# The even layer's norm as a factor of its products, with raw x turned between the first of them, and the output projection's parts two places sooner

## Chip, cores and metric

One core of one Trainium2 chip runs the whole program. The metric is the time of one execution on the device in microseconds (us). TensorE is the matrix engine, ScalarE, VectorE and GpSimd (POOL) work elementwise, and SyncE (SP) issues nearly all DMAs. All data is fp32.

## What is computed

The program runs two blocks on x of 256 tokens by 1024 features. The first block is a gated delta rule mixer (8 query/key heads, 16 value heads of 128, chunks of 64, in both directions) with an output projection of 2048 to 1024, then a mixture of 32 experts, then a gated embedding. The second block is an even layer and an odd layer. What the change touches:

```python
# end of the first block: gated embedding
x = x + sigmoid(layernorm(x) @ pe_w_gate) * (p @ pe_w_proj)
# even layer
xn = rmsnorm(x, g_norm)              # x * rsqrt(mean(x*x) + 1e-6) * g_norm
p = xn @ w_in
q, k, v, o, z_a, gates, u, z_b = _split(p, EVEN_SPLITS)
qk = silu(causal_conv(concat([q, k]), conv_w))       # 4 taps per channel
gates = gates + b_if
# delta rule's mixer ends with
return o.reshape(bsz, seq, GDN_VAL_WIDTH) @ w_out
```

The norm of the even layer is one number for each token, r = rsqrt(mean(x*x) + 1e-6), and one factor for each feature, g_norm. Since r is the same for all features of a token, (r x g) W = r ((x g) W).

## The kernel before

Each engine has its own instruction stream, written out by hand in order; semaphores (`Signal`) tie them together. A "unit" is a weight tile of 1024 by 256, 1 MB, that SP fills into one of 20 slots; `fill` waits until the products of the slot's last unit are done, and `multiplied[s]` and `arrived[s]` count products and fills of slot s. The sixteen slots beyond the first few lie in the arena, in `yt` and in `xt`. One unit's product with all tokens is 16 matmuls of 128x128 by 256 columns; in fp32 each shows as two instructions, so a unit is 32 instructions in the trace, and a 128x128 transpose is two.

**Delta rule** (`gdn_tensor`). The loop over h runs 9 times (h = 0 to 8). In round h TensorE does the levels of head h's triangular inverse and its projections (`project_half`) and, woven in, the four state steps of head h-1: `solve`, `attend`, `add_state`, `read_state`. Each step waits for a copy by ScalarE or VectorE, and the work written between the steps fills those waits. The last round, h = 8, has no projections left; in their place stand the 16 parts of the first half of the output projection: `out_part(cg, part)` takes 4 matmuls (8 instructions) of column group cg; parts 0 and 1 belong to the first token tile, 2 and 3 to the second. Eleven places have 1, 1, 1, 1, 2, 1, 1, 2, 1, 1 and 4 parts, the 4 behind the last `attend`. After the loop comes `out_rest` with the second half of the input rows, with `turn_out(7)` between.

At the end of round 7 the order is solve(6, 3), attend(6, 3), `turn_v(7)` (v of head 7 turned, for the first solve of round 8), with no projection between them, since heads 8 and 9 do not exist. `out_part` waits for the slot's fill, and for the bank's last reader (`out_free`): for the first parts ScalarE's copy of z.

**Experts** (`moe`). 96 units of weights stream through the slots; the rest of the slots' fills follows the products. Then `embed`: gate products in four column groups over two token tiles (banks 4 to 7), p's projection in banks 0 to 3; ScalarE takes the sigmoid of each group, VectorE multiplies and adds to x, group by group (`embedded(1)` to `embedded(4)`).

**Even layer** (`even`). In order: ScalarE waits for `embedded(4)`, squares x with a sum (two instructions), takes Ln and Exp; VectorE makes xn = x r; TensorE turns xn with 16 transposes through two banks (`turn_tensor`), ScalarE copies them out to `xt` with the feature factor g_norm (`turn_scalar`); TensorE makes the gates' products (16 matmuls with 8 columns each) in bank 4, and then 8 units of q and k, one bank each (banks 0 to 3, twice). ScalarE copies each bank to `raw`, VectorE runs the 4 taps of the convolution over it (8 instructions a unit), ScalarE takes silu. VectorE's and ScalarE's steps for the forget gates run beside the units. Then 4 units of v (`project`), the a rows, the scores, and 16 units for z_a, o, z_b and u (`project_on`), each copied by ScalarE with one instruction of 128x512 (Silu for z, Copy for the rest). Everything afterwards stays as it is.

## Time and profile before

| | us |
|---|---|
| three runs | 1200.20, 1204.52, 1205.24 |
| median | 1204.52 |
| the profiled execution's own time | 1200.51 |
| its span | 1199.2 |
| mean granted TensorE clock | 0.95 |

The profiled execution's times below are counted from the start of its span; 1.3 us lie around it. TensorE's rows are split into matmuls (PE) and the weight loads that overlap them (PEld). A row's duration of a matmul contains the time through the pipeline, so a series is read by the step from one start to the next. "idle before <-releaser" is what the engine waited for.

### The profile page before, as it was taken

Reading aid. Unit: us, or ns where it says so; the run is one execution under the profiler, and the core shown is the slowest. Engines: PE = TensorE matmul, PEld = TensorE weight load, DVE = VectorE, ACT = ScalarE, POOL = GpSimd, SP = SyncE. Lnnn points to the kernel's source line nnn. Section 1 sums busy time; section 2 is a strip of 40 time slices with the busy share of each in tenths; the row PEclk is TensorE's granted clock in tenths of the full one; section 3 lists DMA queues with packets and bytes.
Section 4 is the critical chain, followed back from the end, with each engine's and each line's share of the span. In section 5 each row is a group of like instructions: output and inputs, shape, how many; then the busy total and the mean of one; then the engine's idle time right before and its main releaser. Section 6 shows DMA issues by size and latency. Waiting matters only on the chain.

```text
span 1199.2 us, 24296 instructions
## 1 busy us (share of the span) xinstructions
PE 1085.5 (91%) x10653; PEld 831.2 (69%) x10653; DVE 387.6 (32%) x927; ACT 354.8 (30%) x965; POOL 44.3 (4%) x47
## 2 busy tenths in 40 slices
PE   7999999999899989877677979999999798999989
PEld 6776777767667885333233868888888587777877
DVE  2555555555542242110001424411001100074760
ACT  2654655545553221100001131111002500133440
POOL 0110000000000000000000000000000000023000
PEclk9999999999899999898888969999999899799989
DMA  6233233223226568999999413334443234432211
GB/s 257 78 128 116 72 117 118 86 101 122 93 72 267 190 225 346 419 421 422 421 421 419 182 56 140 141 140 140 142 164 115 71 140 177 107 140 71 90 51 36
DMA packets 39887, 210.41 MB, mean 175 GB/s; under 512 B 5200, under 2 KB 14288, under 8 KB 15840
## 3 DMA queue, kind: packets, MB, share of 16 engines
q1 hardware_dynamic: 39776, 208.79, 46.0%
q8 instruction: 87, 1.43, 0.5%
q14 instruction: 24, 0.20, 0.1%
HBM read 207.66 MB, written 1.11 MB: 174 GB/s over the span
## 4 chain that ended last, share of the span: by engine, by line
PE 76%; SPq 10%; DVE 5%; DMA 4%; ACT 4%; issue 2%; DVEq 0%; ACTq 0%
PE ps L448 9%; SPq L235 9%; PE ps L2230 9%; PE ps L250 7%; PE ps L2148 5%; PE ps L451 4%; PE ps L764 3%; DMA arena<-in_wu 2%; PE ps L2611 2%; PE ps L2519 2%; PE ps L2026 2%; PE ps L775 2%; PE ps L2550 2%; PE ps L504 2%; PE ps L470 2%
## 5 line engine op out<-in xcount | busy, mean ns | idle before, releaser
L448 PE MATMUL ps<-xt,slots 128*128 128x256 f32 x512 | 128.0, 397 | 0.0
L2230 PE MATMUL ps<-slots,xt 128*128 128x256 f32 x512 | 110.7, 379 | 0.0
L448 PEld LDWEIGHTS ps<-xt,slots 128*128 128x128 f32 x512 | 95.1, 195 | 19.8 <-issue 7.5
L2230 PEld LDWEIGHTS ps<-slots,xt 128*128 128x128 f32 x512 | 97.2, 190 | 13.2
L1533 PE MATMUL ps<-arena 128*32 128x512 f32 x280 | 54.1, 666 | 22.8 <-DMA arena<-in_wu 9.1
L451 PE MATMUL ps<-slots,xt 128*128 128x256 f32 x256 | 65.1, 398 | 0.0
L250 PE MATMUL ps<-slots,yt 128*128 128x256 f32 x256 | 57.3, 388 | 0.9 <-ACT yt L280 0.9
L2148 PE MATMUL ps<-xt,slots 128*128 128x256 f32 x256 | 57.1, 387 | 0.0
L1087 DVE SCALAR_TENSOR_TENSOR arena<-arena 128x256 f32<-128x256 f32 x128 | 56.3, 486 | 0.3
L250 PEld LDWEIGHTS ps<-slots,yt 128*128 128x128 f32 x256 | 49.8, 195 | 8.4 <-ACT yt L280 1.3
L2148 PEld LDWEIGHTS ps<-xt,slots 128*128 128x128 f32 x256 | 49.7, 195 | 7.0
L451 PEld LDWEIGHTS ps<-slots,xt 128*128 128x128 f32 x256 | 46.9, 193 | 10.8 <-issue 4.3
L1533 PE MATMUL ps<-slots,arena 128*32 128x512 f32 x160 | 44.4, 708 | 6.0 <-DMA xt<-in_wu 6.0
L1533 PEld LDWEIGHTS ps<-arena 128*32 128x32 f32 x280 | 14.8, 120 | 50.4 <-issue 50.4
L2916 POOL TENSOR_TENSOR arena<-arena 128x512 f32<-128x512 f32 (+1 forms) x8 | 17.8, 2259 | 732.1 <-DVE arena L2811 732.1
L2375 DVE SCALAR_TENSOR_TENSOR arena<-ps,arena 128x256 f32<-128x256 f32 x8 | 3.2, 478 | 108.3 <-ACT arena L2285 108.3
L2278 ACT ACTIVATE arena<-ps 128x512 f32<-128x512 f32 x16 | 9.6, 597 | 93.8 <-PE ps L2230 93.8
L1633 ACT ACTIVATE arena<-ps 128x256 f32<-128x256 f32 x8 | 3.1, 385 | 115.1 <-PE ps L1533 115.1
L1309 POOL TENSOR_TENSOR arena<-arena 128x256 f32<-128x256 f32 x32 | 24.8, 776 | 312.1 <-ACT arena L830 194.0
L266 PE MATMUL ps<-cst,arena 128*128 128x128 f32 x84 | 17.5, 370 | 20.5 <-DVE arena L2316 7.7
L1854 DVE TENSOR_TENSOR arena<-arena,ps 128x256 f32<-128x256 f32 x8 | 3.4, 422 | 92.8 <-ACT arena L1633 92.8
L2550 PE MATMUL ps<-slots,xt 128*128 128x256 f32 x128 | 31.8, 393 | 1.2 <-ACT arena L2718 1.2
(386 smaller groups left out, 1853.9 us busy)
## 6 DMA issues: line engine op xcount, KB each, us to landing
slots<-in_wu SPq DMA_DIRECT2D x114, 1024.0 KB, 4.8
arena<-in_wu SPq DMA_DIRECT2D x58, 1024.0 KB, 26.1
yt<-in_wu SPq DMA_DIRECT2D x10, 1024.0 KB, 26.1
xt<-in_wu SPq DMA_DIRECT2D x4, 1024.0 KB, 27.7
arena<-bias_rows SPq DMA_DIRECT2D x1, 2048.0 KB, 14.7
arena<-delta_rows SPq DMA_DIRECT2D x14, 128.0 KB, 7.6
xt<-in_xt SPq DMA_DIRECT2D x2, 512.0 KB, 5.3
x<-in_x SPq DMA_DIRECT2D x1, 1024.0 KB, 8.2
```

The lines of the kernel that those rows point to most:

```text
L235: SP.dma_start(self.slot(slot), self.ins["wu"][unit]).then_inc(*self.arrived[slot].up())
L250: q = M.matmul(self.bank(base + cg, UC, t * UC), lhs[:, h * KT + k, t * P:(t + 1) * P], self.slot(s)[:, k, :], start=(t == 0 and k == 0 an ...
L448: q = M.matmul(bank(n, T), self.slots[:, s, k, n * P:(n + 1) * P], self.xt[:, k, :], start=(k == 0), stop=(k == KT - 1))
L451: q = M.matmul(bank(n, UC), folded(k, n), self.slots[:, s, k, :], start=(k == 0), stop=(k == KT - 1))
L470: q = M.matmul(ps[p, 3, n], g.mt[p, cc, m % 4], g.X[p, cc, m % 4], start=True, stop=True, skip_group_check=True)
L764: q = M.matmul(self.out_bank(t, cg), self.yt[:, k, t * P:(t + 1) * P], self.slots[:, s, k, :], start=((cg % 2 == 0 or (t, cg) == (1, 3)) a ...
L1087: q = V.scalar_tensor_tensor(g.cn[:, s], src, w, g.cn[:, s], ALU.mult, ALU.add)
L1309: G.tensor_tensor(by_cc(g.mt), by_cc(g.ac), g.lvt[:, l].unsqueeze(1).to_broadcast([P, 2, 128]), ALU.mult).then_inc(*g.masked.up())
L1533: q = M.matmul(self.ps[r, 2, :], g.xg[:, half * (KT // 2) + k, r], self.flat(slots[e])[:, k * 512:(k + 1) * 512], start=(half == 0 and k = ...
L2148: q = M.matmul(bank(s, T, T * n), self.slots[:, s, k, n * P:(n + 1) * P], self.xt[:, k, :], start=(k == 0), stop=(k == KT - 1), skip_group ...
L2230: q = M.matmul(self.bank(s, UC, t * UC), self.xt[:, k, t * P:(t + 1) * P], self.slots[:, s, k, :], start=(t == 0 and k == 0), stop=(k == K ...
L2550: q = M.matmul(bank(g.z_banks[u], UC, t * UC), self.xt[:, k, t * P:(t + 1) * P], self.slots[:, u, k, :], start=(t == 0 and k == 0), stop=( ...
```

## The change

*Even layer.* The norm is taken out of the products' input. p's products (all units of the even layer's input projection and the gates') take xe, which is raw x turned, with only the feature factor on it; it lies in `yt` instead of `xt`. The factor of the token comes in behind: for q and k as a multiplication by a row `rrow` (r spread over all partitions with a product of ones by a diagonal matrix, two matmuls, and a copy), done by VectorE as it takes the bank to `raw` in ScalarE's place; for v, z, o and u as the scale of ScalarE's copy, now two instructions of 128x256 with one scale each instead of one of 128x512; for the gates as the scalar of a VectorE instruction. The gates' products are made by feature (8 matmuls with 8 weight columns by 256 moving columns), copied, and turned back by two small transposes, and stand behind the third q,k unit. The turns of raw x stand in `embed_tensor`: part c (two feature tiles) as soon as VectorE has added column group c; part 0 behind the third gate product of the second token tile, parts 1 and 2 behind the fourth, part 3 inside the first q,k unit, whose matmuls are put in the order of the parts. ScalarE's squares of x are taken group by group, between the copies; a load of the joint table for Ln and Exp stands ahead of the last two groups. TensorE waits for `diag_made` behind the first unit. A small DMA of the feature factors (128 rows of 32 bytes) is added at the start of the expert stage. Ahead of VectorE's work only the first three columns of `raw` are cleared.

*Delta rule.* Each part of the output projection stands two places sooner: parts (0, 0) and (0, 1) in round 7, behind solve(6, 3) and behind attend(6, 3); behind the last attend stand two parts instead of four.

```diff
@@ gdn_tensor, last round @@
             if last:
-                self.out_part(0, 0)
+                self.out_part(0, 2)
...
             if h + 2 < QKH:
                 project_half(h + 2, 0, 1)
+            if h == QKH - 1:
+                self.out_part(0, 0)
             if last:
-                self.out_part(2, 3)
+                self.out_part(3, 1)
             if step:
                 attend(h - 1, 3)
             if h + 2 < QKH:
                 project_half(h + 2, 1, 0)
+            if h == QKH - 1:
+                self.out_part(0, 1)
             if level:
                 turn_v(h)
             if h + 2 < QKH:
                 project_half(h + 2, 1, 1)
             if last:
-                for part in range(4):
-                    self.out_part(3, part)
+                self.out_part(3, 2)
+                self.out_part(3, 3)
@@ moe_sync @@
+        SP.dma_start(self.enorm[:, :], I["feat"][:, F_ENORM:F_ENORM + KT]).then_inc(*self.enorm_in.up())
@@ embed_tensor @@
                 if t == 1:
                     q.then_inc(*self.multiplied[s].up())
+                    for c in {2: (0,), 3: (1, 2)}.get(cg, ()):
+                        self.turn_raw(c)
...
+        M.wait_ge(*self.arrived[0](self.multiplied[0].n + 1))
+        for c in range(4):
+            M.wait_ge(*self.raw_kept(c + 1))
+            for n in range(2):
+                for k in (2 * c, 2 * c + 1):
+                    q = M.matmul(self.bank(0, T, T * n), self.slots[:, 0, k, n * P:(n + 1) * P], self.xe[:, k, :],
+                                 start=(n == 0 and k == 0), stop=(k == KT - 1), skip_group_check=True)
+            if c == 0:
+                self.turn_raw(3)
+        q.then_inc(*self.multiplied[0].up())
+    def turn_raw(self, c):
+        M = self.nc.tensor
+        M.wait_ge(*self.embedded(c + 1))
+        for j in range(2):
+            for t in range(NT):
+                q = M.transpose(self.bank(c, P, j * T + t * P), self.x[:, t, (2 * c + j) * P:(2 * c + j + 1) * P],
+                                self.c["ident"])
+        q.then_inc(*self.raw_turned.up())
@@ embed_scalar @@
+        def keep(c):
+            A.wait_ge(*self.enorm_in(1))
+            A.wait_ge(*self.raw_turned(c + 1))
+            for k in (2 * c, 2 * c + 1):
+                q = A.activation(self.xe[:, k, :], self.bank(c, T, k % 2 * T), ACT.Copy, scale=self.enorm[:, k:k + 1])
+            q.then_inc(*self.raw_kept.up())
+        def square(c):
+            A.wait_ge(*self.embedded(c + 1))
+            for t in range(NT):
+                A.activation(g.sg[:, c, t], self.x[:, t, c * UC:(c + 1) * UC], ACT.Square,
+                             accum_out=self.rms[:, 4 * t + c:4 * t + c + 1]).then_inc(*self.squared.up())
+        for cg in range(3):
+            gate(cg)
+        keep(0)
+        square(0)
+        gate(3)
+        keep(1)
+        keep(2)
+        square(1)
+        keep(3)
+        A.preload_act_table_set("natural_log_exp_and_others")
+        square(2)
+        square(3)
@@ even_tensor @@
-        M.wait_ge(*g.xn_made(1))
-        self.turn_tensor(g.xn, KT, [0, 1], g.turned, g.xt_kept)
...
         for i in range(2):
             for s in range(4):
+                if (i, s) == (0, 0):
+                    M.wait_ge(*g.diag_made(1))
+                    for t in range(NT):
+                        q = M.matmul(bank(5, P, t * P), c["ones"], g.diag[:, t], start=True, stop=True,
+                                     skip_group_check=True)
+                    q.then_inc(*g.r_spread.up())
+                    continue
                 if i > 0:
-                    M.wait_ge(*g.raw_kept(s + 1))
+                    M.wait_ge(*g.raw_made(s + 1))
...
+                if (i, s) == (0, 2):
+                    M.wait_ge(*g.loaded(5))
+                    for k in range(KT):
+                        q = M.matmul(self.ps[0:2 * AH, 4, 0:T], g.wif[:, k, :], self.xe[:, k, :], start=(k == 0),
+                                     stop=(k == KT - 1), skip_group_check=True)
+                    q.then_inc(*g.gates_f.up())
+            if i == 0:
+                M.wait_ge(*g.gf_kept(1))
+                for t in range(NT):
+                    q = M.transpose(bank(4, 2 * AH, T + 2 * AH * t), g.gf[0:2 * AH, t * P:(t + 1) * P],
+                                    c["ident"][0:2 * AH, 0:2 * AH])
+                q.then_inc(*g.gates.up())
@@ even_vector @@
+                V.tensor_tensor(g.raw[:, 2 * s:2 * s + 2, 3:3 + T], bank(s).rearrange("p (n t) -> p n t", n=2),
+                                g.rrow[:, :].unsqueeze(1).to_broadcast([P, 2, T]), ALU.mult).then_inc(*g.raw_made.up())
```

## Rows read from the trace of the kernel before

**Rows 1.** The page, part 1: busy time, share of the span, instructions.
```profile
PE 1085.5 (91%) x10653; PEld 831.2 (69%) x10653; DVE 387.6 (32%) x927; ACT 354.8 (30%) x965; POOL 44.3 (4%) x47
```

**Rows 2.** Windows: start:end, length, each engine's busy us, granted clock, DMA share, GB/s.
```profile
362.00:364.00 2.00, 2.00 (x7) 1.63 (x6) 0.00 (x0) 1.79 (x10) 0.00 (x0) 0.50 0.77 291
...
440.00:444.00 4.00, 2.39 (x20) 2.09 (x19) 2.65 (x16) 0.21 (x1) 0.00 (x0) 1.00 1.01 424
...
590.00:610.00 20.00, 10.92 (x76) 3.15 (x80) 1.45 (x3) 0.60 (x1) 0.00 (x0) 0.83 1.02 422
...
696.00:699.00 3.00, 0.00 (x0) 0.00 (x0) 0.00 (x0) 2.95 (x6) 0.00 (x0) 0.50 0.87 300
...
717.00:720.00 3.00, 3.00 (x16) 2.64 (x15) 0.00 (x0) 0.00 (x0) 0.00 (x0) 1.00 0.00 0
```

**Rows 3.** Timeline, gate products to q,k units: start, us, engine, line, operation, [idle before <-releaser].
```profile
668.77 24.34 PE L2026 MATMUL ps<-arena,xt 128*128 128x256 f32 x112
...
694.56 0.69 DVE L2053 TENSOR_TENSOR x<-x,arena 128x512 f32<-128x512 f32 x1
...
697.82 1.28 ACT L2127 ACT_TABLE_LOAD   x1
...
700.83 1.97 PE L266 MATMUL ps<-cst,arena 128*128 128x128 f32 x8 [7.72 <-DVE arena L2316]
...
705.95 7.00 PE L2137 MATMUL ps<-arena,xt 128*128 128x8 f32 x32 [0.93 <-ACT xt L280]
...
712.80 12.40 PE L2148 MATMUL ps<-xt,slots 128*128 128x256 f32 x49
...
724.82 45.06 PE L2148 MATMUL ps<-xt,slots 128*128 128x256 f32 x208
...
770.66 0.80 PE L2156 MATMUL ps<-arena,cst 128*128 128x4 f32 x6 [0.78 <-ACT arena L2254]
```

**Rows 4.** Prices: two timeline rows, then groups by line (busy us, mean ns | idle).
```profile
658.83 0.20 ACT L1668 ACTIVATE arena<-arena 128x1 f32<-128x1 f32 x1
...
659.93 0.86 PEld L1657 LDWEIGHTS ps<-cst,x 128*128 128x128 f32 x8 [1.32 <-DVE x L1702]
...
L250 PE MATMUL ps<-slots,xt 128*128 128x256 f32 x128 | 27.9, 380 | 0.0
...
L280 ACT ACTIVATE yt<-ps,arena 128x256 f32<-128x256 f32 x16 | 6.6, 469 | 1.8 <-PE ps L266 1.7
...
L2342 DVE SCALAR_TENSOR_TENSOR arena<-arena 128x256 f32<-128x256 f32 x12 | 4.9, 481 | 0.0
...
L2381 DVE TENSOR_TENSOR arena<-arena,ps 128x512 f32<-128x512 f32 x4 | 2.7, 687 | 13.6 <-PE ps L2210 13.6
...
L2298 ACT ACTIVATE arena<-arena 128x256 f32<-128x256 f32 x8 | 3.2, 404 | 0.1
...
L2184 PE MATMUL ps<-cst,arena 128*128 128x128 f32 x12 | 1.5, 275 | 0.8 <-ACT arena L2278 0.8
```

**Rows 5.** Timeline, end of the delta rule's round 7 and start of round 8.
```profile
354.86 0.66 PE L523 MATMUL ps<-arena 64*64 64x128 f32 x8
...
357.67 1.12 PE L532 MATMUL ps<-arena 64*64 64x128 f32 x8 [2.14 <-ACT arena L850]
...
360.96 1.12 PE L523 MATMUL ps<-arena 64*64 64x128 f32 x8 [1.13 <-ACT arena L928]
...
362.01 3.17 PE L764 MATMUL ps<-slots,yt 128*128 128x256 f32 x8
...
365.11 0.66 PE L532 MATMUL ps<-arena 64*64 64x128 f32 x8
...
366.35 1.99 PE L764 MATMUL ps<-slots,yt 128*128 128x256 f32 x8
```

**Rows 6.** Timeline, tail of the output projection: last scaling on VectorE, rest on TensorE.
```profile
400.99 1.14 DVE L1200 SCALAR_TENSOR_TENSOR arena<-arena 128x128 f32<-128x128 f32 x4 [5.09 <-ACT arena L959]
...
402.38 7.93 PE L775 MATMUL ps<-slots,yt 128*128 128x256 f32 x36
```

More of the change, by code:

```diff
@@ L2033, in embed_tensor, with gate @@
         g.projected = [self.multiplied[s].last() for s in GATE_SLOTS]
+        M.wait_ge(*self.arrived[0](self.multiplied[0].n + 1))
[8 more added lines that the diff above has]
+        q.then_inc(*self.multiplied[0].up())
+        self.first_unit = self.multiplied[0].last()
+    def turn_raw(self, c):
[6 more added lines that the diff above has]
+        q.then_inc(*self.raw_turned.up())
     def embed_scalar(self, g):
         A = self.nc.scalar
-        for cg in range(4):
+        def gate(cg):
             A.wait_ge(*g.projected[cg])
@@ L2260, in even_scalar @@
             A.wait_ge(*g.projected[cg])
-            A.activation(g.pj[:, 0, :, cg * UC:(cg + 1) * UC], bank(cg).rearrange("p (t n) -> p t n", t=NT),
-                         ACT.Copy).then_inc(*g.kept.up())
+            for t in range(NT):
+                q = A.activation(g.pj[:, 0, t, cg * UC:(cg + 1) * UC], bank(cg, UC, t * UC), ACT.Copy,
+                                 scale=r[:, t:t + 1])
+            q.then_inc(*g.kept.up())
         A.wait_ge(*g.a_rows(1))
@@ L2277, in even_scalar @@
                 :, (i % 8 // 4) * 2:(i % 8 // 4) * 2 + 2, (i % 4) * UC:(i % 4 + 1) * UC]
-            A.activation(dst, bank(i % 4).rearrange("p (t n) -> p t n", t=NT),
-                         ACT.Silu if i < 8 else ACT.Copy).then_inc(*g.kept.up())
+            for t in range(NT):
+                q = A.activation(dst[:, t], bank(i % 4, UC, t * UC), ACT.Silu if i < 8 else ACT.Copy,
+                                 scale=r[:, t:t + 1])
+            q.then_inc(*g.kept.up())
         for b in range(3):
@@ L2343, in even_vector @@
                                 *(g.convolved if tap == 3 else g.tap).up())
+            if i == 0:
+                V.wait_ge(*g.gates(1))
+                for t in range(NT):
+                    q = V.scalar_tensor_tensor(g.gt[:, t], bank(4, 2 * AH, T + 2 * AH * t), r[:, t:t + 1], g.bif[:, :],
+                                               ALU.mult, ALU.add)
+                v(q)
+                V.scalar_tensor_tensor(g.l2[:, :, :], fg, -1.0, fg, ALU.mult, ALU.max).then_inc(*g.abs_made.up())
+                V.wait_ge(*g.soft_ln(1))
+                V.scalar_tensor_tensor(g.lf[:, :, :], fg, 0.0, g.l2[:, :, :], ALU.min, ALU.subtract).then_inc(
+                    *g.lf_made.up())
         V.wait_ge(*g.sums(1))
```

111 lines of the change are left out of this document (53 added, 58 removed).

## The prediction

> **What bounds the kernel now.** I read the page first: TensorE is busy for nine tenths of the span [rows 1], so an edit counts where it takes TensorE's idle time, its slow time or its work away. Then I read the windows with clock and DMA share. In the expert stage (590 to 610 stands for it) the DMA engines are full, at 422 GB/s, and TensorE is busy for 10.92 of 20 us; every other stage that the change touches has DMA to spare. In the windows 362 to 364 and 696 to 699 the granted clock is 0.50, the 1.2 GHz level; by 717 to 720 it is 1.00, 2.4 GHz [rows 2]. Then the timeline at both places. At the even layer TensorE ends the gate products at 693.11, idles 7.72 us while the norm is worked out, turns x at the slow clock, runs the 32 gate instructions from 705.95 for 7.00 us and begins the first q,k unit at 712.80 [rows 3]. From there to 769.88 it is dense. At the end of the delta rule's seventh head it idles 2.14 us for ScalarE, and 1.13 us again before 360.96 [rows 5]. These two gaps and the slow stretches behind them are what can be won.
>
> **Even layer: prices.** At 2.4 GHz a unit of 32 instructions takes 27.9 us / 4, less the tail of the last one, 6.91 us; one 256-column instruction is 0.216 us. Eight transposing instructions (four turns, in fp32 two instructions each) take 0.87 us: the loads of the eight span 0.86 us. A ScalarE copy with a scale of 128x256 takes 6.6 us / 16 = 0.41, I take 0.42 us, a square of that size 0.40 us. VectorE's product of a 512-column bank is 0.69 us, a tap step 0.48 us [rows 4].
>
> **Even layer: TensorE's new course**, in the times of before. Gate products end at 693.11; what follows is four turns of raw x (3.5 us, one of them ahead of the last gate product) and p's first q,k unit (6.91 us) woven in. Each wait in there is early enough. The last add of x is at 694.56 + 0.69 = 695.25 [rows 3]; with the one turn moved ahead of it some 696.2, while its turn is issued only at 693.11 + 3 x 0.87 + 1.73 = 697.5. ScalarE's copies of parts 1 and 2 end at about 695.9 and 696.8, needed at 698.4 and 700.1; part 3's at 699.5, needed at 701.9. So the first unit ends at 693.11 + 3.5 + 6.91 = 703.5.
>
> The wait that is added stands right behind it, diag_made ahead of the two norm-spreading products; behind it in TensorE's queue stand all other units. ScalarE: copy of part 3 until 699.45, table load 1.28 [rows 3], four squares 1.6 plus the accumulator's last read 0.2 (an estimate from the step of the squares), so 702.5. VectorE's sum 0.2, Ln and Exp some 0.5 (Exp 0.20 us, no table load ahead of it once the joint set is there [rows 4]), two 128x128 products some 0.4, and 0.2 for semaphores: 703.8. The stall is then 0.3 us; its bounds are nothing (chain a little shorter) and 2 us (each step a little longer). The spreading is four 128-column instructions, 0.44 us. The next unit starts at 704.2 instead of 721.6.
>
> Seven units are 48.4 us: 752.6. The gates by feature are 8 products of 256 columns, 16 instructions, 3.46 us where 7.00 stood; turning them back is some 0.3 us. So the eighth unit ends at 756.4 against 724.82 + 45.06 = 769.88: **13.5 us sooner**. In short: 7.7 us of idle time and the rest of the serial chain go, the slow clock goes (about 4 us over the gates' products and 1.9 us over the first unit), 0.8 us of spreading and turning comes.
>
> VectorE now takes the units out of the banks: 0.69 + 8 x 0.48, at most 4.5 us a unit, against 6.91 that TensorE needs. ScalarE loses its eight copies. Behind the eighth unit TensorE waits for VectorE's 0.69 instead of ScalarE's 0.60; the 0.78 us of idle [rows 3] become 0.85. The copies of values, z and the rest become two scaled ones of 0.42 instead of one of 0.60 us, hidden behind 6.91 us, save the last one ahead of the turned weights, where TensorE idled 0.78 us [rows 4]: 0.25 more. So **13.2 us** remain; bounds 10.5 (the stall at its upper end, and a semaphore here and there) and 14.
>
> The added DMA (128 rows of 32 bytes) is issued on SP ahead of two expert fills, some 0.4 us that nobody waits for: those units are the nineteenth and twelfth. It costs nothing; without that cover it would be the 0.4 us. The larger inputs of the even layer go out 1 us later on SP, with the last add of x. VectorE needs them first, for the taps at about 705, and could catch up 2.4 us a unit; TensorE needs the gate weights at 718.
>
> **Delta rule's end.** The parts are 8 instructions, 1.73 us each. Fourteen places keep their number of parts; two parts leave the tail (3.47 us) for two new places in the eighth head's round. The first falls into the 2.14 us of idle [rows 5]: 355.45 to 357.2, ahead of the 357.62 at which u is there. That place is free. The second stands ahead of the turning of v: attend ends at 358.26, the part at 360.0, turn_v at 360.5 rather than 359.8; behind it come ScalarE's copy (0.84) and the solve, at 361.7 instead of 360.96. This delay is 0.75 us, but the clock: before, the solve, the turns and the first part (3.17 us on the row where 1.99 is the full-clock row) ran at half clock, behind the idle 2.14 us [rows 5]. With the gap filled the clock should stay at its upper level: part (0,2) then ends at 364.05 and the first attend of the last round starts at 364.1 instead of 365.11. So 1.0 us sooner there, 3.5 us off the tail: **4.5 us**. From there to the tail TensorE had work between all waits, the same amount as before. In the tail it is bound by its own work too: o is scaled at 400.99 + 1.14 = 402.13, the turning that waits for it is at 402.38 + 36 x 0.216 = 410.15 [rows 6]; with both moved, 401.1 and 405.7, still in that order. Low bound: the clock falls all the same, the second part costs 3.5 us ahead of turn_v, and 0.5 us is left; high bound 5.
>
> **Does it pass the expert stage?** The full DMA stretch is set off by TensorE's first expert products, which free slots, and ends by bytes. It shifts as a whole with its start, if the DMA was not already behind there. The row at 440 to 444, ahead of it, is routing work on VectorE (2.65 of 4 us busy) with the weights of the first step long asked for [rows 2], so I take the whole 4.5.
>
> **The sum.** 13.2 + 4.5 = 17.7 us. The profiled execution has a span of 1199.2 and took 1200.51, which gives 1182.8. The three runs are 1200.2, 1204.52 and 1205.24; their median lies 4.0 us above the profiled one, which gives 1186.8. I take 1186, since two of three runs were of the longer kind.
>
> **A rule against it.** The one stretch of the trace that has transposes behind an idle stretch, 700.83 on, stays at 0.50 through them and through narrow products [rows 2, 3], while the eight transposes at 659.93 stand among dense products at full clock [rows 4]. The Trainium skill, page "TensorE: Matmul & The Clock Gate", section "Part 4: PE-mode transpose", says that transposes do not count as busy for the gate. By it, the 1.7 us of two turns in a row plus the stall could drop the clock, and the second rival's time would hold. The trace leaves both open; that is why that rival has its chance.
>
> **The rivals.**
> First: the delta rule's 4.5 us do not come through, because the second part delays turn_v at half clock, or because the DMA stretch in the expert stage starts no sooner. For it: the granted clock there was 0.50 and the chain solve, copy, solve is serial; DMA is full at 590 to 610 and all around it. Against: the idle that preceded the drop is filled. It gives 1186 + 4 = 1190.
> Second: TensorE's clock falls at the wait for diag_made and the turns, and stays low for a while. For: the delta rule's 2.14 us of idle were enough for some 8 us of half clock, which cost about 4 us. Against: 1.6 of 4 us without a product left it at 1.00 in 440 to 444 [rows 2]. My stall of 0.3 us would have to be near 2. It gives 1186 + 2 + 4 = 1192.
> Third, on the other side: VectorE becomes the bound of the q,k units. TensorE's units five to eight wait for its product into raw. Its turn is 3.7 to 4.5 us against 6.91; only beyond 6.91 does it cost at all, over eight units, and the 17.7 us are eaten when a turn takes 9.1 us. At 10 us, 8 x 3.1 = 25 us, it gives 1211. Only a doubled price of reading the bank or of the spread operand would do it, and the 512-column row with a bank operand has 687 ns [rows 4].
> Fourth: raw x isn't taken in between p's products, as one of the copies comes late, and TensorE idles in the weave. Each of the three copies has 2.4 us or more to spare by the times above, so one would have to be 4 to 5 us later for the 3 us that this costs; it gives 1189.
>
> **How the numbers follow.** Forecast 0.66, first rival 0.15, second 0.09, fourth 0.07, third 0.02; 0.01 for something else. The forecast's own range is 1181 to 1189, from the two kinds of runs and the bounds of the terms. To leave out no more than 2 in 10 the range goes from 1180 to 1192. A measurement of this kernel can tell about 0.5%, 6 us, from no change. All cases but the third are faster by more than that: faster 0.96, same 0.02, slower 0.02.
>
> **What would show it.** In the profile after: no idle beyond 0.5 us on TensorE from the gate products to the eighth unit but the one at the spreading products, and a granted clock of 1.00 there; gate products' end to eighth unit's end 63.3 us instead of 76.8; at the last two heads no 0.50 window, and 16 instructions of parts in the tail where 32 stood; start of the expert products 4.5 us sooner and the DMA-bound stretch of the same length. It would be wrong if the stall at diag_made is over 1 us, if the window behind it has a clock below 1, if VectorE has no idle between units, or if the expert products start sooner and end as late as before.

## The result, and the profile after

| us | before | after |
|---|---|---|
| runs | 1195.68, 1200.20, 1204.52, 1205.24 | 1179.04, 1179.33, 1180.10, 1183.65 |
| median | 1202.36 | 1179.71 |
| profiled execution's own time | 1200.51 | 1179.04 |
| its span | 1199.2 | 1177.4 |
| mean granted TensorE clock | 0.950 | 0.962 |

The run of 1195.68 of the kernel before is a fourth beside the three that the prediction had. The changed kernel takes 0.983 of the time before, 95% interval 0.980 to 0.986. The forecast was 1186, so the direction and most of the size were right. The measured median lies 6 us below it and 0.3 us below the lower end of the range. The profiled executions differ by 21.8 us of span, where the sum had 17.7. All times and windows below are in us from the start of the span of their own kernel, and line numbers are that kernel's own.

The page of the kernel after, busy time, against [rows 1]:

```profile
PE 1076.1 (91%) x10643; PEld 821.0 (70%) x10643; DVE 391.3 (33%) x937; ACT 354.0 (30%) x988; POOL 43.8 (4%) x47
```

TensorE's busy time fell by 9.4 us only, and the span by 21.8: more than half of the gain was idle time. The rest is work at half clock and the gates' products.

The timeline after, from the gate products to the end of the q,k units, against [rows 3]. L2036 are the gate products, L2064 the turns of raw x, L2051 the first q,k unit, L2196 the spreading of r, L2205 the other units, L2212 the gates by feature, L2225 the gates' sums:

```profile
663.22 20.88 PE L2036 MATMUL ps<-arena,xt 128*128 128x256 f32 x96
...
683.94 0.60 PE L2064 MATMUL ps<-cst,x 128*128 128x128 f32 x4
684.38 3.62 PE L2036 MATMUL ps<-arena,xt 128*128 128x256 f32 x16
687.83 1.04 PE L2064 MATMUL ps<-cst,x 128*128 128x128 f32 x8
688.70 1.89 PE L2051 MATMUL ps<-yt,slots 128*128 128x256 f32 x8
690.43 0.60 PE L2064 MATMUL ps<-cst,x 128*128 128x128 f32 x4
690.87 5.34 PE L2051 MATMUL ps<-yt,slots 128*128 128x256 f32 x24
...
696.32 0.71 PE L2196 MATMUL ps<-arena,cst 128*128 128x128 f32 x4
696.87 13.98 PE L2205 MATMUL ps<-yt,slots 128*128 128x256 f32 x64
710.77 3.62 PE L2212 MATMUL ps<-yt,arena 128*8 128x256 f32 x16
714.33 7.17 PE L2205 MATMUL ps<-yt,slots 128*128 128x256 f32 x32
...
721.64 27.89 PE L2205 MATMUL ps<-yt,slots 128*128 128x256 f32 x128
...
750.41 0.80 PE L2225 MATMUL ps<-arena,cst 128*128 128x4 f32 x6 [0.88 <-DVE arena L2405]
```

Each row starts where the one above it ends, less the overlap of the pipeline. The idle 7.72 us and the stretch of turns and gates behind it are gone. Read by steps: from the start of the gate products to the start of the gates' sums it is 750.41 - 663.22 = 87.19 us, where it was 770.66 - 668.77 = 101.89 [rows 3].

The wait for diag_made shows on the weight load of the spreading; behind it the windows of that stretch (start:end, length, busy PE, PEld, DVE, ACT, POOL, granted clock, DMA share, GB/s), against 696 to 699 in [rows 2]:

```profile
696.32 0.52 PEld L2196 LDWEIGHTS ps<-arena,cst 128*128 128x128 f32 x4 [0.50 <-DVE arena L2391]
```

```profile
692.00:696.00 4.00, 4.00 (x20) 3.37 (x18) 0.38 (x3) 3.47 (x11) 0.00 (x0) 1.00 0.95 371
696.00:699.00 3.00, 2.90 (x15) 2.45 (x15) 0.69 (x4) 0.39 (x1) 0.00 (x0) 1.00 0.59 182
```

The timeline after, end of the delta rule's round 7, against [rows 5]. L524 is the solve, L769 a part of the output projection, L533 attend, L568 the turning of v:

```profile
353.96 0.66 PE L524 MATMUL ps<-arena 64*64 64x128 f32 x8
354.55 1.99 PE L769 MATMUL ps<-slots,yt 128*128 128x256 f32 x8
356.77 0.66 PE L533 MATMUL ps<-arena 64*64 64x128 f32 x8 [0.23 <-ACT arena L855]
357.36 1.99 PE L769 MATMUL ps<-slots,yt 128*128 128x256 f32 x8
359.19 0.60 PE L568 MATMUL ps<-cst,arena 128*128 128x128 f32 x4
360.92 0.66 PE L524 MATMUL ps<-arena 64*64 64x128 f32 x8 [1.13 <-ACT arena L933]
...
363.43 0.66 PE L533 MATMUL ps<-arena 64*64 64x128 f32 x8
```

Of the idle 2.14 us 0.23 are left, and the solve and the parts keep their full-clock durations (0.66 and 1.99, where [rows 5] have 1.12 and 3.17). The wait of 1.13 us ahead of the next solve stands as before.

**Where the 21.8 us came from.** I cut the span at five marks that all kernels have: the solve (6, 3) of round 7, the start of the long `out_rest` group, the first expert product, the start of the long group of gate products, and the gates' sums. Each number is the difference of two starts on TensorE's timeline:

| stretch, us | before | after | gain |
|---|---|---|---|
| start to solve (6, 3) | 354.86 | 353.96 | 0.90 |
| to `out_rest` (delta rule's end) | 47.52 | 43.28 | 4.24 |
| to the first expert product | 47.57 | 47.57 | 0 |
| to the gate products (experts) | 218.82 | 218.41 | 0.41 |
| to the gates' sums (even layer) | 101.89 | 87.19 | 14.70 |
| to the end | 428.54 | 426.99 | 1.55 |

The two changed stretches give 18.9 us. The other 2.9 us come from stretches that the change leaves alone, save 0.24 us that it costs in the last one; the experiments show that these stretches differ from execution to execution.

### The profile page after: what moved, and what is told of

Read it like the earlier page. It is cut to its first block, busy times and chain, and to the rows that moved or that the text cites. A ratio compares the mean times of both kernels' runs of the same rounds, so it can differ in the third digit from the quotient of the medians.

```text
span 1177.4 us, 24312 instructions
## 1 busy us (share of the span) xinstructions
PE 1076.1 (91%) x10643; PEld 821.0 (70%) x10643; DVE 391.3 (33%) x937; ACT 354.0 (30%) x988; POOL 43.8 (4%) x47
## 4 chain that ended last, share of the span: by engine, by line
PE 76%; SPq 10%; DVE 5%; ACT 4%; DMA 3%; issue 2%; ACTq 0%; DVEq 0%
SPq L236 10%; PE ps L2299 9%; PE ps L449 9%; PE ps L251 7%; PE ps L452 4%; PE ps L2205 4%; PE ps L2695 3%; PE ps L769 2%; PE ps L2603 2%; PE ps L780 2%; PE ps L2036 2%; DMA arena<-in_wu 2%; PE ps L2634 2%; PE ps L505 2%; PE ps L1541 2%
## 5 line engine op out<-in xcount | busy, mean ns | idle before, releaser
L449 PE MATMUL ps<-xt,slots 128*128 128x256 f32 x512 | 127.1, 395 | 0.0
L2299 PE MATMUL ps<-slots,yt 128*128 128x256 f32 x512 | 110.7, 379 | 0.0
L449 PEld LDWEIGHTS ps<-xt,slots 128*128 128x128 f32 x512 | 94.7, 194 | 19.6 <-issue 7.5
L2299 PEld LDWEIGHTS ps<-slots,yt 128*128 128x128 f32 x512 | 97.2, 190 | 13.2
L251 PE MATMUL ps<-slots,yt 128*128 128x256 f32 x384 | 83.4, 379 | 1.0 <-ACT yt L281 1.0
L251 PEld LDWEIGHTS ps<-slots,yt 128*128 128x128 f32 x384 | 72.8, 190 | 11.0 <-ACT yt L281 1.2
L1541 PE MATMUL ps<-arena 128*32 128x512 f32 x280 | 56.5, 693 | 23.4 <-DMA arena<-in_wu 9.1
L452 PE MATMUL ps<-slots,xt 128*128 128x256 f32 x256 | 64.5, 395 | 0.0
L452 PEld LDWEIGHTS ps<-slots,xt 128*128 128x128 f32 x256 | 46.5, 192 | 10.6 <-issue 4.3
L2205 PE MATMUL ps<-yt,slots 128*128 128x256 f32 x224 | 49.0, 380 | 0.0
L2205 PEld LDWEIGHTS ps<-yt,slots 128*128 128x128 f32 x224 | 42.3, 190 | 6.1 <-issue 0.4
L2347 ACT ACTIVATE arena<-ps,rms 128x256 f32<-128x256 f32 x32 | 13.4, 471 | 90.2 <-PE ps L2299 90.2
L2634 PE MATMUL ps<-slots,xt 128*128 128x256 f32 x128 | 31.9, 395 | 1.2 <-ACT arena L2802 1.2
L769 PE MATMUL ps<-slots,yt 128*128 128x256 f32 x128 | 31.0, 389 | 0.0
## 6 DMA issues: line engine op xcount, KB each, us to landing
arena<-bias_rows SPq DMA_DIRECT2D x1, 2048.0 KB, 14.7
```

The source lines that it names most:

```text
L251: q = M.matmul(self.bank(base + cg, UC, t * UC), lhs[:, h * KT + k, t * P:(t + 1) * P], self.slot(s)[:, k, :], start=(t == 0 and k == 0 an ...
L449: q = M.matmul(bank(n, T), self.slots[:, s, k, n * P:(n + 1) * P], self.xt[:, k, :], start=(k == 0), stop=(k == KT - 1))
L452: q = M.matmul(bank(n, UC), folded(k, n), self.slots[:, s, k, :], start=(k == 0), stop=(k == KT - 1))
L769: q = M.matmul(self.out_bank(t, cg), self.yt[:, k, t * P:(t + 1) * P], self.slots[:, s, k, :], start=((cg % 2 == 0 or (t, cg) == (1, 3)) a ...
L1541: q = M.matmul(self.ps[r, 2, :], g.xg[:, half * (KT // 2) + k, r], self.flat(slots[e])[:, k * 512:(k + 1) * 512], start=(half == 0 and k = ...
L2205: q = M.matmul(bank(s, T, T * n), self.slots[:, s, k, n * P:(n + 1) * P], self.xe[:, k, :], start=(k == 0), stop=(k == KT - 1), skip_group ...
```

## The experiments

**One half at a time.** The first two kernels separate the halves.

e1 takes the even layer of the kernel after, with every part of the output projection back in its old place:

```
             if last:
-                self.out_part(0, 2)
+                self.out_part(0, 0)
...
-            if h == QKH - 1:
-                self.out_part(0, 0)
...
-            if h == QKH - 1:
-                self.out_part(0, 1)
```

> The even layer's change alone; the delta rule's parts stand where they stood before. My theory (two independent gains): from the first 112-instruction group of gate products to the end of the eighth q,k unit 86.3 us as in the changed kernel instead of 101.1, so 14.8 us, and 0.3 to 0.9 given back behind it: a span 14 us below the kernel before, and the first expert products not sooner than before (449.9). Rival (the parts' gain is lost in the expert stage's DMA stretch and all 21.8 us come from the even layer): a span 19 to 22 us below.

Measured: median 1182.55 (1181.09 to 1183.28), against 1202.72 of before beside it; ratio 0.984, interval 0.981 to 0.987. Span 1181.6. The even stretch is 87.20 us, the same as in the kernel after; the delta rule's stretch 47.55, the same as before. The span is 17.6 us below before, where the theory had 14 and the rival 19 to 22. By stretches 14.69 of them are the even layer; 0.80, 0.46 and 1.68 lie in the first, the fourth and the last stretch, which that forecast left out.

e2 is the other half: the kernel before with the 16 parts at their places of the kernel after:

```
+            if h == QKH - 1:
+                self.out_part(0, 0)
             if last:
-                self.out_part(2, 3)
+                self.out_part(3, 1)
...
+            if h == QKH - 1:
+                self.out_part(0, 1)
             if level:
                 turn_v(h)
```

> The delta rule's parts alone, the even layer as before. My theory: the clock window 358 to 364 is at 1.00, the first attend of the last round some 0.8 to 1.7 us sooner, the tail 3.46 us shorter, the first expert products at 444.8 to 445.8, and the same 4 to 5 us at the start of the gate products and at the end: 4 to 5 us faster than before. Rival (the full DMA stretch ends where it did): expert products sooner, gate products at 668 as before, no change in the span.

Measured: median 1198.22 (1192.76 to 1200.67), ratio 0.997, interval 0.995 to 0.999. Its delta rule stretch is 43.27 us and its even stretch 101.85. So the halves don't disturb each other, and each is worth in its stretch what it is worth in both kernels: 14.7 and 4.2 us. The 4.25 us also come through the expert stage behind them: from the mark at its start to the gate products e2 takes 218.71 us against 218.82. The first rival (the gain swallowed by full DMA) falls. The span is 7.7 us below before, but 3.5 of that lie in the first stretch, ahead of the edit.

Two windows of e1 show what the delta half removes, columns as above:

```profile
356.00:358.00 2.00, 1.15 (x9) 0.82 (x10) 0.03 (x1) 0.80 (x3) 0.00 (x0) 0.74 0.00 0
358.00:360.00 2.00, 0.97 (x4) 0.56 (x4) 0.39 (x1) 0.84 (x2) 0.00 (x0) 0.50 0.00 0
```

and one of the kernel after at the same place:

```profile
358.00:360.00 2.00, 1.79 (x11) 1.34 (x9) 0.00 (x0) 0.18 (x1) 0.00 (x0) 1.00 0.00 0
```

**Which of the two parts pays.** e3 leaves part (0, 1) out of round 7, so that three parts remain in the tail:

```
-            if h == QKH - 1:
-                self.out_part(0, 1)
...
             if last:
+                self.out_part(3, 1)
                 self.out_part(3, 2)
                 self.out_part(3, 3)
```

> The changed kernel with one part only in the seventh-to-eighth round: part (0, 0) stays in the gap behind solve(6, 3), part (0, 1) and all others one place sooner than before, three parts in the tail. Separates the two parts. My theory: the first fills an idle gap and keeps the clock up, the second costs 0.7 us by delaying the turning of v and gives 1.73 us in the tail. So the first attend of the last round comes about 1.8 us sooner than in the changed kernel (361.6 on its scale), the expert products about 0.0 to 0.1 us sooner or up to 0.5 later; the span within 0.5 us of the changed kernel. Rival (it is the second part that holds the clock up in the gap between turning v and the solve): a granted clock of 0.50 appears in the windows from 358 to 364, and the expert products are 2 to 4 us later than in the changed kernel.

Measured: median 1179.71 (1177.43 to 1180.78), ratio 0.982, interval 0.979 to 0.985, the same as the kernel after. Timeline of e3 at the same place:

```profile
354.44 0.66 PE L568 MATMUL ps<-cst,arena 128*128 128x128 f32 x4
356.39 0.66 PE L524 MATMUL ps<-arena 64*64 64x128 f32 x8 [1.29 <-ACT arena L932]
```

From solve (6, 3) to the first attend of round 8 it is 7.84 us here and 9.47 in the kernel after: the second part delays the first attend of round 8 by 1.63 us, and it takes 1.73 us off the tail. Its stretch is 43.37 us against 43.28, so the second part is worth 0.1 us and the first one all of the rest. With the first part alone the granted clock is 1.00 in all windows from 351 to 361.

**The same two parts, better placed.** e4 puts the second part behind the turning of v, where TensorE idles 1.13 us for ScalarE's copy, and the spreading of r behind the second q,k unit in place of the first:

```
-            if h == QKH - 1:
-                self.out_part(0, 1)
             if level:
                 turn_v(h)
+            if h == QKH - 1:
+                self.out_part(0, 1)
...
-                    M.wait_ge(*g.diag_made(1))
-                    for t in range(NT):
-                        q = M.matmul(bank(5, P, t * P), c["ones"], g.diag[:, t], ...)
-                    q.then_inc(*g.r_spread.up())
...
                 g.qk_done.append(self.multiplied[s].last())
+                if (i, s) == (0, 1):
+                    M.wait_ge(*g.diag_made(1))
+                    for t in range(NT):
+                        q = M.matmul(bank(5, P, t * P), c["ones"], g.diag[:, t], ...)
+                    q.then_inc(*g.r_spread.up())
```

> The changed kernel with two moves: part (0, 1) stands behind the turning of v instead of ahead of it, and the two norm-spreading products with their wait stand behind the second q,k unit instead of ahead of it. My theory: the solve waits for the turning, ScalarE's copy and nothing else, the part fills that wait, so the solve comes 1.3 us sooner than in the changed kernel; and TensorE has no idle at the spreading (0.5 us less), while VectorE starts 6.9 us later and catches up 3.1 us a unit before anyone waits for it. Sum 1.8 us faster than the changed kernel in the profile (span near 1175.6), which the times alone can hardly show. Rival (VectorE's late start makes TensorE wait for a bank at the fifth unit, or for the eighth product): an idle of 1 us or more on TensorE between the fourth and the ninth unit.

Measured: median 1175.65 (1174.91 to 1181.10), ratio 0.980, interval 0.977 to 0.983; the lowest median of this study, though its slower runs overlap with the kernel after's. Timeline of e4 in round 7, then at the even layer (L2200 the units, L2207 the spreading):

```profile
354.16 0.66 PE L568 MATMUL ps<-cst,arena 128*128 128x128 f32 x4
354.66 1.89 PE L769 MATMUL ps<-slots,yt 128*128 128x256 f32 x8
356.48 0.66 PE L524 MATMUL ps<-arena 64*64 64x128 f32 x8
...
693.39 7.07 PE L2200 MATMUL ps<-yt,slots 128*128 128x256 f32 x32
700.29 0.61 PE L2207 MATMUL ps<-arena,cst 128*128 128x128 f32 x4
700.74 7.07 PE L2200 MATMUL ps<-yt,slots 128*128 128x256 f32 x32
```

The 1.13 us of idle are gone; the delta stretch is 42.03 us, 1.25 less than after. At the even layer no idle is left and the stretch is 86.83 us, 0.36 less. VectorE starts on the banks later, and that cost nothing. The remaining 1.6 us of the span's 3.2 are not from the edits: e4 had a start to solve (6, 3) of 350.77 us (3.19 less), which its routing stretch (49.20 against 47.57) gives back half of.

**Does the weave pay?** e5 makes all turns of raw x behind the last gate product, with the copies and then the first unit behind them, and no turn between products. ScalarE makes all four copies ahead of all its squares, which the excerpt leaves out:

```
-                    for c in {2: (0,), 3: (1, 2)}.get(cg, ()):
+                    for c in {3: (0, 1, 2, 3)}.get(cg, ()):
                         self.turn_raw(c)
...
         for c in range(4):
-            M.wait_ge(*self.raw_kept(c + 1))
+            M.wait_ge(*self.raw_kept(4))
...
-            if c == 0:
-                self.turn_raw(3)
```

> The changed kernel without the weave: all four turns of raw x stand behind the last gate product, TensorE's first q,k unit waits for all four copies, and ScalarE squares after the copies. It measures what it is worth to turn x between p's products. My theory: TensorE idles 3 to 4 us from the last turn to the fourth copy, the clock falls to 0.50 behind it for some microseconds (3 us more), and the stall at the diagonal is hidden or small: 5 to 7 us slower than the changed kernel. Rival (the clock stays up, as the turns and a short idle do not bring it down): 3 to 4 us slower.

Measured: median 1183.48 (1175.39 to 1187.20), ratio 0.984, interval 0.979 to 0.989. The whole time tells little here; the stretch does. It is 89.25 us, so the weave is worth 2.06. Timeline of e5:

```profile
691.86 1.47 PE L2062 MATMUL ps<-cst,x 128*128 128x128 f32 x12
694.22 0.66 PE L2062 MATMUL ps<-cst,x 128*128 128x128 f32 x4 [0.89 <-DVE x L2112]
695.96 7.14 PE L2051 MATMUL ps<-yt,slots 128*128 128x256 f32 x32 [1.08 <-ACT yt L2079]
```

Two waits of 0.89 and 1.08 us are all that comes in place of the weave, and the clock stays at 1.00 in all windows from 690 to 705. The expectation missed: it had 3 to 4 us of idle in one piece and a fall of the clock, and even its rival had 3 to 4 us in all. Of the 14.7 us 12.6 are thus the rest of the even layer's change, above all the norm as a factor of the products, whose chain no longer stands ahead of the first unit; 2.1 are the weave. No run separates the gates' new form from the 12.6. By an estimate it is worth nothing by itself: the 32 instructions took 7.00 us [rows 3] in windows that all have a clock of 0.50 (705 to 714), which at the full clock would be 3.5, and the new form takes 3.56 and 0.21 for the turning back.

**VectorE as the bound.** e6 lets VectorE make the product out of the bank seven times in each unit (six results thrown away):

```
+                for _ in range(6):
+                    V.tensor_tensor(g.pj[:, 4, 0, 0:2 * T]..., bank(s)..., g.rrow..., ALU.mult).then_inc(*g.extra.up())
+                    V.wait_ge(*g.extra.last())
```

> The changed kernel with six more VectorE products of the bank by the spread row (into a part of the arena that is unused then) for each of the eight q,k units, so that VectorE's turn is about 3.75 + 6 x 0.73 = 8.1 us against TensorE's 6.91. It tests where VectorE would become the bound. My theory: the cost is only what VectorE lacks from its first product at 698.75 on: its eighth product into raw ends near 698.8 + 7 x 8.1 + 6 x 0.73 + 0.7 + 1 = 762, where it was at 750.3, so 11 to 13 us slower. Rival (the cover is larger or the spread operand costs nothing more): under 4 us slower.

Measured: 1193.63, one run; span 1192.0, even stretch 98.08 us, 10.9 more. Timeline of e6:

```profile
726.04 27.89 PE L2206 MATMUL ps<-yt,slots 128*128 128x256 f32 x128
...
756.88 0.69 DVE L2411 TENSOR_TENSOR arena<-ps,arena 128x512 f32<-128x512 f32 x1
...
764.85 0.69 DVE L2411 TENSOR_TENSOR arena<-ps,arena 128x512 f32<-128x512 f32 x1
765.69 1.42 PE L2226 MATMUL ps<-arena,cst 128*128 128x4 f32 x6 [11.76 <-DVE arena L2411]
```

A turn of VectorE is 764.85 - 756.88 = 7.97 us here against 6.9 of a unit on TensorE. In the kernel after it is 0.69 + 0.62 + 2.46, some 3.8 us. The bill doesn't come where the third rival had it: TensorE's units run without a gap (27.89 us, as before), because the four banks buffer the lag, and the whole of it is paid behind the eighth unit, in a wait of 11.76 us where the kernel after has 0.88. VectorE begins at 703.27, TensorE's last unit ends at 753.9, and 1.4 us of VectorE's time between the fourth and the fifth unit go to the gates. TensorE waits for the product of the eighth turn and not for the 2.9 us of taps behind it. So, as an estimate, a turn could be (753.9 + 0.7 - 703.3 - 1.4 + 2.9) / 8 = 6.6 us before anything is lost; at 7.97 it gives 11.0 us of loss, where 10.9 were measured. The mechanism of the rival exists; it was 2.8 us a unit away from deciding.

**The wait for diag_made, longer.** e8 and e9 add three and seven squares on ScalarE ahead of the last groups' squares (results thrown away), so that only the wait grows. The edit of e9; that of e8 has a 3 for the 7:

```
         A.preload_act_table_set("natural_log_exp_and_others")
+        A.wait_ge(*self.squared(4))
+        for _ in range(7):
+            A.activation(g.sg[:, 1, 0], self.x[:, 0, UC:2 * UC], ACT.Square).then_inc(*g.extra.up())
+            A.wait_ge(*g.extra.last())
```

> The changed kernel with seven more squares of 128x256 on ScalarE ahead of the last two groups, which make the wait for the diagonal about 0.5 + 7 x 0.45 = 3.6 us long. It tests the rival in which TensorE's clock falls at this wait. Theory A (an idle of this length brings it down, as 2.14 us did in the delta rule before): 3.1 us by the wait and 3 to 4 us by a slow stretch behind it, 6 to 7 us in all. Theory B (dense products around it keep it up): 3.1 us and no window below 0.9 but the one with the idle itself.

> The kernel after with three extra squares of 128x256 on ScalarE ahead of the last two groups' squares (work added, results thrown away), so that the sum of squares comes later and TensorE's wait at diag_made behind the first q,k unit grows from 0.50 us to some 1.7 us (seven extra squares made it 3.24). Both theories have the wait itself cost 1.2 us more. Theory A, that an idle stretch of this length is still harmless, as the 1.6 of 4 us without a product were in the routing stretch: granted clock 1.00 in every window behind it, the next two units in 14.0 us, gate group to gate-sum products 87.2 + 1.2 = 88.4 us. Theory B, that this length is enough, as the 2.14 us of the delta rule were: a window near 0.7 or below behind it, the two units in about 15.5 us, 90 us from the gate group to the gate-sum products.

Measured: e8 1186.42 (span 1184.8), e9 1187.24 (span 1185.9), one run each. The timeline and a window of e8:

```profile
701.62 0.71 PE L2201 MATMUL ps<-arena,cst 128*128 128x128 f32 x4 [1.44 <-DVE arena L2396]
702.17 13.98 PE L2210 MATMUL ps<-yt,slots 128*128 128x256 f32 x64
```

```profile
701.00:704.00 3.00, 2.38 (x13) 2.17 (x14) 1.52 (x5) 0.44 (x2) 0.00 (x0) 1.00 0.99 320
```

The timeline and two windows of e9:

```profile
701.65 0.71 PE L2201 MATMUL ps<-arena,cst 128*128 128x128 f32 x4 [3.24 <-DVE arena L2396]
702.20 15.67 PE L2210 MATMUL ps<-yt,slots 128*128 128x256 f32 x64
```

```profile
701.00:704.00 3.00, 2.35 (x10) 2.00 (x11) 1.50 (x5) 0.47 (x2) 0.00 (x0) 0.77 0.52 218
704.00:707.00 3.00, 3.00 (x11) 2.44 (x10) 2.85 (x8) 0.00 (x0) 0.00 (x0) 0.66 0.00 0
```

With 1.44 us of idle the next two units take 13.98 us as in the kernel after, and the stretch is 88.54 us, 1.35 more, which is the added wait (6.78 us between the start of the first unit's last 24 instructions and the spreading, 5.45 in the kernel after). With 3.24 us the clock falls, the two units take 1.69 us more, and the stretch is 92.03 us: 3.13 of wait, 1.7 of slow clock. Theory A of e9 had the fall right and its price too high (3 to 4 us). So the second rival's mechanism is real; the wait of the kernel after, 0.50 us, did not set it off. Each length was profiled once, and the stretches below show that the same wait can end either way, so these runs give no length from which the clock falls.

**Transposes and the clock.** The prediction left open whether a run of transposes would let the clock fall. e7 puts 80 more of them between the first unit and the wait for diag_made (results overwritten):

```
+        for n in range(80):
+            M.transpose(self.bank(3, P, n % 4 * P), self.x[:, n % 2, (n % 8) * P:(n % 8 + 1) * P], self.c["ident"])
```

> The changed kernel with 80 more transposes of x (into a bank that is unused then) between the first q,k unit and the wait for the diagonal. It tests whether a stretch of transposes alone keeps TensorE's clock up. Theory A (transposes keep it up): 80 x 0.108 = 8.6 us, less the stall of 0.5 us that they cover: 8.1 us slower, all windows at 1.00. Theory B (transposes do not count as busy): the granted clock falls to 0.50 within the stretch, the rest of them take 0.22 us each and the next unit begins slow: 12 to 20 us slower.

Measured: 1187.61, one run; span 1185.9, even stretch 95.56 us, 8.37 more. Timeline and a window of e7:

```profile
694.31 8.90 PE L2058 MATMUL ps<-cst,x 128*128 128x128 f32 x80
...
703.49 13.98 PE L2207 MATMUL ps<-yt,slots 128*128 128x256 f32 x64
```

```profile
700.00:703.00 3.00, 3.00 (x30) 3.00 (x29) 0.00 (x0) 0.00 (x0) 0.00 (x0) 1.00 0.00 0
```

For 8.7 us TensorE does nothing but transposes, and the granted clock stays at 1.00 in them and behind them, while 3.24 us of idle at the same place let it fall in e9. Here a run of transposes keeps the clock up as a run of products does. The Trainium skill, page "TensorE: Matmul & The Clock Gate", section "Part 4: PE-mode transpose", says that transposes don't count as busy for the clock gate. By it e7 should have lost its clock. The measurement decides, for fp32 transposes of 128x128.

The 80 show as 80 instructions, 0.109 us each. That corrects a price of the prediction, below.

**What differs without a cause in the code.** The stretches of all kernels, from the same marks:

| us | start to solve (6, 3) | to out_rest | to experts | to gate products | to gates' sums | to the end |
|---|---|---|---|---|---|---|
| before | 354.86 | 47.52 | 47.57 | 218.82 | 101.89 | 428.54 |
| after | 353.96 | 43.28 | 47.57 | 218.41 | 87.19 | 426.99 |
| e1 | 354.06 | 47.55 | 47.57 | 218.36 | 87.20 | 426.86 |
| e2 | 351.35 | 43.27 | 47.57 | 218.71 | 101.85 | 428.75 |
| e3 | 351.06 | 43.37 | 47.57 | 219.42 | 87.20 | 429.28 |
| e4 | 350.77 | 42.03 | 49.20 | 218.55 | 86.83 | 426.82 |
| e5 | 354.55 | 43.28 | 50.46 | 219.39 | 89.25 | 428.47 |
| e6 | 354.63 | 43.28 | 50.43 | 219.27 | 98.08 | 426.31 |
| e7 | 351.99 | 43.27 | 47.57 | 218.65 | 95.56 | 428.86 |
| e8 | 354.13 | 43.27 | 50.51 | 219.27 | 88.54 | 429.08 |
| e9 | 354.60 | 43.28 | 49.08 | 218.45 | 92.03 | 428.46 |

Three columns jump between levels with no relation to the edits. The chip is not what sets them: e1 to e4 ran on one chip, e5, e6, e7 and e9 on a second and e8 on a third, and on each of the first two both levels occur. In the first column, the longer executions have a piece of "issue" in the chain of waits near 255 (time in which TensorE waited for nothing that the profile shows) of 2.09 to 2.42 us; e7 has 1.24, e3 and e4 0.93, e2 none. That of the kernel after, and the window behind it:

```profile
255.11 2.10 issue
```

```profile
258.00:262.00 4.00, 4.00 (x19) 2.37 (x16) 3.02 (x11) 0.00 (x0) 0.00 (x0) 0.64 0.02 6
```

In all seven executions with the long piece the granted clock of that window is 0.57 to 0.64; in e2, e3, e4 and e7 it is 1.00. Between the kernel after and e4 the gap explains 1.2 of the 3.19 us, and the slow stretch behind it 1.6 more. Why the gap is there stays open.

In the third, the routing between experts and projection has waits of 1.31 and 0.78 us for VectorE in every kernel, and the 32 gathering products (L1522) behind them take 3.84 us in the kernel after (start 439.34) and 6.78 in e8 (start 439.50). The window with them, kernel after and then e8:

```profile
440.00:444.00 4.00, 3.30 (x31) 3.21 (x29) 2.08 (x11) 2.55 (x5) 0.00 (x0) 1.00 0.02 4
```

```profile
440.00:444.00 4.00, 4.00 (x21) 4.00 (x21) 1.50 (x9) 0.67 (x2) 0.00 (x0) 0.50 0.02 6
```

The same waits leave the clock at 1.00 in one execution and bring it down in another. The last column is alike: behind the even layer's mixer TensorE idles 3.40 us, and the clock comes back sooner or later. The timeline of the kernel after, then the first window in which TensorE is dense again, kernel after and before:

```profile
927.17 1.97 PE L267 MATMUL ps<-cst,arena 128*128 128x128 f32 x8 [3.40 <-ACT yt L281]
```

```profile
936.00:940.00 4.00, 4.00 (x20) 3.54 (x19) 0.00 (x0) 0.00 (x0) 0.00 (x0) 1.00 0.00 0
```

```profile
956.00:960.00 4.00, 4.00 (x14) 3.28 (x14) 0.00 (x0) 0.00 (x0) 0.00 (x0) 0.71 0.00 0
```

It is worth some 1.5 to 3 us. Of the nine kernels with the new even layer, four have the lower level of 426.3 to 427.0 us (after, e1, e4, e6) and five the upper of 428.5 to 429.3 (e3, e5, e7, e8, e9), as before and e2 have, so the gain of 1.55 us in the last stretch is not an effect of the change that these profiles show. What sets the level in an execution stays open.

## Why the prediction was right, and where it was off

**What bounds the kernel, and where the gain lies**: right. The 7.72 us are gone, 0.23 are left of the 2.14, and no slow window is left behind either; the 1.13 us stand, and only e4 fills them.

**Even layer**: 13.2 forecast, 14.46 measured (14.70 to the gates' sums, and 0.24 lost at the turned weights). The mis-sized term is the price of the turns. I read the rows of eight transposes as four and had each as two instructions, as an fp32 product is. A transpose is one instruction: L2064 has x4 for a `turn_raw`, and two of them together take 0.87 us. So four turns cost 1.75 us, not 3.5, and the first unit ended some 1.8 us sooner than forecast. The statement in the section on the kernel before, that a 128x128 transpose is two instructions, is wrong for the same reason. The wait at diag_made came out as forecast in spite of it (0.50 us on the weight load; on the products 5.45 - 24 x 0.216 = 0.27, against 0.3), because ScalarE's chain starts from the last of those turns and was sooner by about the same. Since both sides of the wait moved together, its agreement is luck and checks neither. Small terms went the other way: the spreading took 0.55 us for 0.44, the gates by feature 3.56 for 3.46, two units 13.90 for 13.82, and about as much again lies in the last four units and the waits beside them. So 13.5 + 1.75 less some 0.5 is the measured 14.70.

**The turned weights**: the idle ahead of them went from 0.78 to 1.02 us, 0.24 more where 0.25 was forecast:

```profile
L2253 PE MATMUL ps<-cst,arena 128*128 128x128 f32 x12 | 1.5, 275 | 1.0 <-ACT arena L2347 1.0
```

**Covered costs**: VectorE's products out of the banks, the copies in two, the added DMA and the later inputs cost nothing that shows. VectorE did wait 2.27 us for the layer's inputs, until 698.53, and TensorE lost nothing by it; e6 gives the distance to the bound for the first of them.

**Delta rule**: 4.5 forecast, 4.24 measured: 0.78 us at the start of round 8 (forecast 1.0) and the two parts off the tail (3.47). The reason was right, the clock stayed at 1.00 (the window above; all from 354 to 366 show it). The weak step is the price of the second part. The prediction set the new order against before (solve (7, 0) at 361.7 instead of 360.96) and called the 0.75 us the second part's delay. That sum came out: from solve (6, 3) to that solve it is 6.96 us after, forecast 361.7 - 354.86 = 6.84, and 6.10 before [rows 5]. But the kernel to compare with is the one with the first part alone, and e3 has 5.33: the first part had already won 0.77 by the clock, and the second puts 1.63 back, nearly its full length of 1.73. The first part alone is worth 4.15 us of the 4.24 and the second 0.1; that the forecast's total came near is in part because it set the second part's delay against the clock's gain in one number. The second part stands in a chain turn of v, copy, solve that nothing covers. Behind `turn_v` it lies beside the copy (e4).

**The expert stage** shifted whole, as forecast.

**The level.** The sum against the profiled execution gave 1182.8, and the profiled execution of the kernel after took 1179.04: 3.8 us lower, which by spans is 4.1 us: 1.26 of the even layer, 0.9 and 0.4 of the first and the fourth stretch and 1.8 of the last, less 0.26 of the delta rule. Of these only the even layer's and the delta rule's are steps of the sum; the rest is the spread of the stretches. The single step that missed most is the level that I put on top: 1186 is 3.2 us above 1182.8, because two of three runs were of the longer kind. The median of the kernel after, with runs of 1179.0, 1179.3, 1180.1 and 1183.7, is 0.7 above its profiled execution, and before's, over 17 runs beside e1, is 1202.72, 2.2 above. That step put the forecast 2.5 us too high, and the range's lower end came to lie 0.3 us above the median.

**Rivals.** First (gain lost at the delta rule or in the experts): not so, e2. Second (clock falls at diag_made): no; 1.44 us of wait did not do it in e8, 3.24 did in e9. Third (VectorE): no; its turn is some 3.8 us, it idles 1.5 us or more between units, and e6 shows how far the bound is. Fourth (weave late): no copy was late; e5 shows that all of the weave is 2.06 us.

## What to carry to other kernels

A norm's factor per token can be taken behind the products that it feeds; what that is worth is the whole chain that stood ahead of the first product, its idle and the slow clock behind it (12.6 of 14.7 us here, all else that came with it included), while weaving the turns gave another 2.1. A filler belongs behind the step whose copy is awaited, not ahead of it: the same eight instructions were worth 0.1 us on one side of `turn_v` and 1.25 more on the other. And a kernel's time is best compared stretch by stretch between marks on the bounding engine; three stretches here jump by 1.5 to 4 us on their own, as much as many an edit is worth.

## What the runs showed of the hardware

- A transpose of 128x128 in fp32 shows as one instruction at 0.109 us (80 in 8.7 us), an fp32 product of 128 by 256 as two of 0.216.
- A run of 80 fp32 transposes kept the granted clock at 1.00 (e7).
- In the even layer 0.50, 0.89 with 1.08, and 1.44 us of idle kept it (after, e5, e8), 3.24 us did not (e9); at the end of the delta rule's round 7 2.14 us did not (before, e1); near 255 us 0.93 and 1.24 did (e3, e4, e7), 2.09 and more did not (seven executions). In the routing stretch the same two waits left it up in six of the eleven profiled executions and brought it down in five (third column).
